# Expert weights of a mixture layer streamed in transfers of 2 MB instead of 1 MB

## What is computed

```python
def moe_swiglu(x2d, w_router, w_gate, w_up, w_down):   # 8 experts, 2 for each token
    ...
    def expert_block(args):
        xb, e = args
        return (jax.nn.silu(xb @ w_gate[e]) * (xb @ w_up[e])) @ w_down[e]
    ...
    y = jax.ops.segment_sum(y_rows[dest] * w_sorted[:, None], tok_sorted, num_segments=n_tok)
    return y.astype(x2d.dtype)

...
f = moe_swiglu(u2.reshape(b * s, d), moe_router[i // 2], moe_wg[i // 2],
               moe_wu[i // 2], moe_wd[i // 2]).reshape(b, s, d)
h = h + f
e = rms_norm(p[i] @ ple_proj[i], ple_norm_g[i])
h = h + jax.nn.sigmoid(h @ ple_gate[i]) * e
```

## Time and profile before

| | us |
|---|---|
| median of three runs | 3133.54 |
| lowest and highest | 3129.72, 3134.11 |
| the profiled execution, first to last instruction (its span) | 3126.8 |

### The profile page before, as it was taken

The page is one execution under the profiler, slowest core; times in us unless marked ns, Lnnn a source line. Parts: engine busy times, 40 slices in busy tenths (PEclk is TensorE's granted clock), DMA queues, the critical chain, the costliest instruction groups (busy, mean ns, idle before and its releaser), DMA issues. The chain is left out here.

```text
span 3126.8 us, 47318 instructions
## 1 busy us (share of the span) xinstructions
PE 3067.2 (98%) x18746; PEld 1808.6 (58%) x18746; DVE 1953.1 (62%) x3355; ACT 797.4 (26%) x2086; POOL 162.0 (5%) x146
## 2 busy tenths in 40 slices
PE   8999999999999999999999999999999999999998
PEld 7858686784468577785685576864433333333333
DVE  7766785774577544633575536432477786677777
ACT  4514452441335143221352223231200000000000
POOL 0000000000000002300001104110100000000000
PEclk9999999999999999999999999999999999999999
DMA  7442145344324440133444421133799999999993
GB/s 296 187 181 110 54 173 214 138 163 181 144 98 178 161 183 28 68 115 137 173 171 175 172 81 67 56 142 125 292 405 419 420 418 420 365 417 418 419 419 133
DMA packets 81048, 665.55 MB, mean 213 GB/s; under 512 B 10528, under 2 KB 11168, under 8 KB 14016
## 3 DMA queue, kind: packets, MB, share of 16 engines
q1 hardware_dynamic: 78816, 655.41, 52.9%
q10 hardware_dynamic: 2016, 7.13, 0.6%
HBM read 661.46 MB, written 1.05 MB: 212 GB/s over the span
## 5 line engine op out<-in xcount | busy, mean ns | idle before, releaser
L4400 PE MATMUL psum<-ring,arena 128*32 128x512 f32 x5376 | 582.2, 592 | 0.0
L4400 PEld LDWEIGHTS psum<-ring,arena 128*32 128x32 f32 x5376 | 175.3, 110 | 400.7 <-issue 399.8
L887 PE MATMUL psum<-ring,arena 128*128 128x256 f32 x1760 | 398.1, 379 | 0.8 <-DVE arena L988 0.8
L887 PEld LDWEIGHTS psum<-ring,arena 128*128 128x128 f32 x1760 | 334.1, 190 | 47.0 <-DVE ring L1001 1.2
L887 PE MATMUL psum<-ring,xT_norm 128*128 128x256 f32 x1320 | 303.0, 379 | 1.7 <-DMA ring<-in_ffn_w 1.7
L942 ACT ACTIVATE arena<-arena 32x128 f32<-32x128 f32 x880 | 269.6, 306 | 31.7 <-DVE arena L1076 22.1
L1001 DVE TENSOR_TENSOR ring<-ring 128x1024 f32<-128x1024 f32 x220 | 267.2, 1215 | 10.0 <-DMA ring<-in_ffn_w 3.4
L887 PEld LDWEIGHTS psum<-ring,xT_norm 128*128 128x128 f32 x1320 | 250.4, 190 | 35.7 <-DMA ring<-in_ffn_w 1.9
L4554 ACT ACTIVATE arena<-psum 128x256 f32<-128x256 f32 x84 | 32.5, 387 | 781.4 <-PE psum L4400 781.4
L907 PE MATMUL psum<-ring,arena 128*128 128x512 f32 x440 | 205.8, 592 | 0.0
L3253 PE MATMUL psum<-xT_norm,ring 128*128 128x256 f32 x832 | 184.1, 380 | 0.0
(11 more groups left out here) (647 smaller groups left out, 3945.3 us busy)
## 6 DMA issues: line engine op xcount, KB each, us to landing
ring<-in_moe_w SPq DMA_DIRECT2D x340, 1024.0 KB, 9.3
ring<-in_ffn_w SPq DMA_DIRECT2D x50, 2048.0 KB, 7.4
ring<-in_ffn_w SPq DMA_DIRECT2D x65, 1024.0 KB, 5.0
ring<-in_merge_w SPq DMA_DIRECT2D x16, 2048.0 KB, 8.5
ring<-in_feat_w SPq DMA_DIRECT2D x12, 2048.0 KB, 9.3
ring<-in_ev_in_w SPq DMA_DIRECT2D x4, 2048.0 KB, 8.9
ring<-in_od_in_w SPq DMA_DIRECT2D x4, 2048.0 KB, 9.6
ring<-in_merge_w SPq DMA_DIRECT2D x8, 1024.0 KB, 11.5
```

Of the source, the lines that this page charges most:

```text
L887: last = pe.matmul(psum[:, bank, 0:GROUP], a[:, k, :], w[:, k, :], start=(fresh and k == 0), stop=(k == KT // 2 - 1), skip_group_check=True)
L4400: last = pe.matmul(psum[part(j), r, :], xg[:, u.i, u.group // GROUPS, r * P + BLOCK * j:r * P + BLOCK * (j + 1)], m[:, j, :], start=(u.i = ...
```

## The change

Units are loaded two at a time: `mixture_loads` lists (first unit, count), two units where the first falls on places 0, 2, 4 or 6, one for place 8, and one for the last unit, which has no follower. `mixture_stream` lays the two units of a pair next to each other in each partition, so that one transfer brings 2 MB, 16 KB to a partition. SyncE waits for the release of the later of the two places' old units, and a pair's landing counts on the semaphore of its first place alone; TensorE and VectorE wait for that. `ple_gate` comes in two pairs in the same way, the first of which waits for both of its places.

```diff
--- before.py
+++ after.py
@@ -216,10 +216,21 @@
     return units
 
 
+def mixture_loads():
+
+    total, loads, i = len(mixture_units()), [], 0
+    while i < total:
+        n = 2 if i % UNIT_SLOTS < UNIT_SLOTS - 1 and i + 1 < total else 1
+        loads.append((i, n))
+        i += n
+    return loads + [(total, 2), (total + 2, 2)]
+
+
 def mixture_stream(gate, up, down, last):
 
 
-    out = np.empty((len(mixture_units()) + 4, P, QUAD, BANK), np.float32)
+    total = len(mixture_units()) + 4
+    out = np.empty((total, P, QUAD, BANK), np.float32)
     for at, (group, kind, i) in enumerate(mixture_units()):
         q, g = group // GROUPS, group % GROUPS
         for j in range(QUAD):
@@ -234,7 +245,8 @@
         w = pack(last[:, c * BANK:(c + 1) * BANK])
         for half in range(2):
             out[len(mixture_units()) + 2 * c + half] = w[:, 4 * half:4 * half + 4]
-    return out.reshape(-1, P, QUAD * BANK)
+    out = out.reshape(total, P, QUAD * BANK)
+    return np.concatenate([out[i:i + n].transpose(1, 0, 2).ravel() for i, n in mixture_loads()])
 
 
 def lay_out(inp):
@@ -4228,6 +4240,7 @@
 
 SHARES, TAKEN, PLACED, TABLE = 5, 12, 14, 21
 SLOT_AT = (14336, 16384, 4096, 6144, 0, 2048, 8192, 10240, 12288)
+assert all(SLOT_AT[i + 1] == SLOT_AT[i] + UNIT for i in range(0, UNIT_SLOTS - 1, 2))
 AHEAD = 4
 
 
@@ -4260,18 +4273,27 @@
         self.prog.load("router", self.router.rearrange("p k e -> p (k e)"), self.prog.inp["router"], sp)
         self.side.load_first(sp, self.mem)
 
+    def slots(self, i, n):
+        at = SLOT_AT[i % UNIT_SLOTS]
+        return self.prog.ring[:, at:at + n * UNIT]
+
+    def piece(self, i, n):
+        return self.stream[i * P * UNIT:(i + n) * P * UNIT].rearrange("(p c) -> p c", p=P)
+
     def first_units(self, sp, branch_sum):
-        for i in range(AHEAD):
+        for i in range(0, AHEAD, 2):
             if i == 2:
                 sp.wait_ge(branch_sum, 12)
-            sp.dma_start(self.slot(i), self.stream[i]).then_inc(self.prog.unit_loaded[i], 16)
+            sp.dma_start(self.slots(i, 2), self.piece(i, 2)).then_inc(self.prog.unit_loaded[i], 16)
 
     def run(self):
         prog, stream, gain, side, mem, router, slot = (
             self.prog, self.stream, self.gain, self.side, self.mem, self.router, self.slot)
         psum = prog.psum
         units = mixture_units()
+        in_pairs = stream.rearrange("(g p c) -> g p c", p=P, c=2 * UNIT)
         groups = NE // QUAD * GROUPS
+        first_of = {j: i for i, n in mixture_loads() for j in range(i, i + n)}
         loads = [len(range(s, len(units), UNIT_SLOTS)) for s in range(UNIT_SLOTS)]
         W = QUAD * BLOCK * ROUNDS
         parts = mem.take(3 * TB * D // 2).bitcast(BF16).rearrange("p (m b d) -> p m b d", m=3, b=TB)
@@ -4356,21 +4378,23 @@
             def _(sp):
                 n_passes = passes(sp)
                 with sp.Fori(0, n_passes) as k:
-                    after = sp.value_load(table[0:1, 1:1 + MAX_PASSES][:, bass.ds(k, 1)], min_val=0, max_val=len(units))
+                    after = sp.value_load(table[0:1, 1:1 + MAX_PASSES][:, bass.ds(k, 1)], min_val=0, max_val=len(units) // 2)
                     sp.wait_ge(pass_open, k + 1)
-                    for i in range(AHEAD, len(units)):
+                    for i, n in mixture_loads():
+                        if i < AHEAD or i >= len(units):
+                            continue
                         if i >= UNIT_SLOTS:
-                            wait_released(sp, k, i - UNIT_SLOTS)
-                        sp.dma_start(slot(i), stream[i]).then_inc(prog.unit_loaded[i % UNIT_SLOTS], 16)
-                    for i in range(AHEAD):
-                        wait_released(sp, k, (loads[i] - 1) * UNIT_SLOTS + i)
-                        sp.dma_start(slot(i), stream[bass.ds(after + i, 1), :, :].rearrange("g p c -> p (g c)"))\
+                            wait_released(sp, k, i + n - 1 - UNIT_SLOTS)
+                        sp.dma_start(self.slots(i, n), self.piece(i, n)).then_inc(prog.unit_loaded[i % UNIT_SLOTS], 16)
+                    for i in range(0, AHEAD, 2):
+                        wait_released(sp, k, max((loads[j] - 1) * UNIT_SLOTS + j for j in (i, i + 1)))
+                        sp.dma_start(self.slots(i, 2), in_pairs[bass.ds(after + i // 2, 1), :, :].rearrange("g p c -> p (g c)"))\
                           .then_inc(prog.unit_loaded[i], 16)
 
             @ph.block.tensor
             def _(pe):
                 def wait_unit(k, i):
-                    s = i % UNIT_SLOTS
+                    s = first_of[i] % UNIT_SLOTS
                     pe.wait_ge(prog.unit_loaded[s], k * (16 * loads[s]) + 16 * (i // UNIT_SLOTS + 1))
 
                 def gather(k, q):
@@ -4591,7 +4615,7 @@
                     last.then_inc(hidden_turned, 1)
 
                 def wait_unit(k, i):
-                    n = i % UNIT_SLOTS
+                    n = first_of[i] % UNIT_SLOTS
                     dve.wait_ge(prog.unit_loaded[n], k * (16 * loads[n]) + 16 * (i // UNIT_SLOTS + 1))
 
                 def mix_rows(k, g):
@@ -4693,8 +4717,8 @@
                 do(dve.tensor_scalar(more[:, 0:1], most, float(CAP), None, ALU.is_gt),
                    dve.tensor_scalar(more[:, 1:2], most, float(2 * CAP), None, ALU.is_gt))
                 do(dve.scalar_tensor_tensor(table_f[:, 0:1], more[:, 0:1], 1.0, more[:, 1:2], ALU.add, ALU.add),
-                   dve.tensor_scalar(table_f[:, 1:3], more, float(-len(units)), float(len(units)), ALU.mult, ALU.add),
-                   dve.tensor_scalar(table_f[:, 3:4], more[:, 0:1], 0.0, float(len(units)), ALU.mult, ALU.add))
+                   dve.tensor_scalar(table_f[:, 1:3], more, float(-len(units) // 2), float(len(units) // 2), ALU.mult, ALU.add),
+                   dve.tensor_scalar(table_f[:, 3:4], more[:, 0:1], 0.0, float(len(units) // 2), ALU.mult, ALU.add))
                 do(dve.tensor_copy(table, table_f))
                 assert do.n == TABLE, do.n
                 dve.tensor_copy(counts[:, 0:1], most).then_inc(pass_open, 1)
```

## The result

The changed kernel takes 3191.15 us (median of five runs, 3183.17 to 3208.56) where the kernel before, on the same chip, takes 3132.92 (3129.72 to 3134.11): a ratio of 1.020, 95% interval 1.0174 to 1.0223. Measured once more, in the last series of experiments, it takes 3184.87 for 3132.10, ratio 1.0176, 1.0159 to 1.0193. So it is slower by 52.8 to 58.2 us. The forecast was 3151, 17.5 us slower than its reference of 3133.54, and its range ended at 3166.

The account below looks back on a forecast made before the run. TensorE sets the pace, with the DMA 0.15 us per group faster. Terms 6.3 + 7.2 + 1.5 + 1.0 + 1.1 - 0.5 = 16.6, rounded to 17: span 3144, with 6.7 around it 3151 us; range 3136 to 3166.

Parts of the forecast that it names:

- T4 past +2.74: VectorE's weight sum T4 ending over 2.74 us after a mixed group's down part starts makes TensorE wait one for one.
- R1: Rival: in the mixture the DMA rate won lets the backlog drain and no group waits; 3132 us, chance 0.12.
- R4: Rival: engines cut 16 KB rows to 8 KB, pairs late by 0.3 us more; 3157 us, chance 0.57 together with the forecast.
- R3: Rival: strays don't count, only waits of kind C and the ends; 7.6 us, 3141 us, chance 0.12.
- R2: Rival: each pair needs 8.0 us with nothing ahead; 30 us, 3163 us, chance 0.12.
- Step (4): Lumps: queued pairs delay tight landings in the mixture, one wait of 0.9 us per three groups, 6.3 us in all.
- step (5): Strays: 0.4 us per group lost in the DMA besides the steps, three quarters counted, 7.2 us, first groups 1.5 more.
- C: Mixed groups pairing the first two and last two down units; the latter pair lands 0.9 us late.
- A: Mixed groups with the second down unit alone and the last two paired; 8.35 us to landing after C's shift, in time.
- B: Mixed groups pairing the middle two down units, and the fourth with an up unit; in time after C's shift.
- limit of 8.4: In A and C, the pair of the last two down units may take 8.4 us from issue to landing.
- The ends: Last mixed group 1.0 us and the gate's later loads 1.1 us, less half a microsecond that before already waits.

Follow-up runs that it names:

- e4: The changed kernel, but VectorE's weight sums read constants and wait for no landing; 3131.52 us, ratio 1.0002.
- e3: The changed kernel's 2 MB transfers with joint landing and later release, but from the old HBM layout in rows of 8 KB; 3190.87 us, ratio 1.0192.
- e13: The changed kernel, but the weight sums of kind C groups alone read constants and wait for no landing; 3173.72 us, ratio 1.0157.
- e1: The changed kernel's HBM layout, but transfers of 1 MB, each with its own release and semaphore; 3131.49 us, ratio 1.0001.
- e2: The changed kernel, but a pair released late goes out as two 1 MB transfers, each with its own semaphore; 3139.88 us, ratio 1.0027.
- e9: As e2, but whoever uses a unit waits for both units of its pair; 3187.23 us, ratio 1.0181.

## Why the prediction was right and wrong

**Right: the place and the chain.** In the mixture TensorE waits for VectorE's L4643 and L4657 and for nothing else of weight, the sums wait for landings, T4 past +2.74 costs one for one, the up units have room (e4), the layout is worth nothing, packets are of 16 KB, R1 doesn't come (no group ends T4 before +2.74, save the one behind the pure half). The sign and the path stand. R4 is out by e3: rows of 8 KB make no difference. R3, at 3141, is out too. R2 came nearest, 3163, with each pair 0.7 us slower from an empty queue; but what was missing isn't only there.

**Wrong: the size, 14.5 us for the 24 periods where 50.4 and 49.5 were measured, or 48 more than in before.** (14.5 is the sum's 6.3 + 7.2 + 1.5 less the half microsecond of before.) Step (4) had the state of the queue and the effect of a wait wrong, and step (5) the strays.

*Step (4), the head of C's chain "behind an idle queue".* It isn't idle. 1.5 us of work are still there, in the run where only C waits, and a surcharge of 1.4 comes on top. Where it alone waits, C is late by 2.7 to 4.0 us, not by 0.9.

*Step (4), "C's wait shifts the issues", so that A and B are in time.* In the earlier trace rows a down part takes 9.44 us; TensorE's wait falls inside it, part of it (1.26 us in the group of 2342.76) ahead of the release of d1, and all of it ahead of those of d2 and d3. So the head of the next chain is shifted along with its tight pair. In the changed kernel the next pair after 2343.0 is issued at 2351.34, 8.3 us later, in a queue that has just run dry; it takes 8.3 us for 7.3, and A's d2+d3 behind it takes 9.5 us for the limit of 8.4 (windows 2351.3:2351.5 and 2363.2:2363.4):

```profile
ring<-in_moe_w SPq DMA_DIRECT2D x1, 2048.0 KB, 8.3
...
ring<-in_moe_w SPq DMA_DIRECT2D x1, 2048.0 KB, 9.5
```

So a wait is bought back in part, where the prediction had it bought back in full. By e13, C's 18.5 us of waits take 7 to 9 us off A (24.0 without them, 14.9 and 16.8 with them) and nothing off B (16.2 without them, 16.9 and 13.9 with them, where the two traces of one kernel are 3 us apart). The rest is lost to the shifted head and to the short queue that makes the next pair dear; and with C freed A is late by 2.3 to 4.4 us in each group and B by up to 4.2, where the prediction without C's shift has 0.9.

*Step (5), strays as a rate.* The 0.4 us per group came from times to landing that rose by 1.5 us in 160 us of before, and were taken to fall at random, the same with pairs as without. They don't. On average they are larger where the queue is short, and in three traces with single transfers (before, e1, e2) it holds over 3 us of work for 832 of the 970 transfers of 1 MB. In the changed kernel's trace all surcharges together are 73 us, in before's 20. With the table in place of the rate the same arithmetic gives 44. The service of 4.88 and the 6.95 from landing to T4 stand.

*The ends.* The last mixed group was put at 1.0 us; its wait grew by 2.5 and in the repeated run by 3.4. The gate was put at 1.1 us: a wait of 3.1 where single loads leave 1.2, so 1.9, and 3.0 more where the clock fell. Group 12, at 1.6, had no term of its own.

The 6.7 us that the forecast set around the span are for the greater part a difference between runs: where time and span of one execution are both listed they are 1.8 to 1.9 us apart (3204.34 and 3202.5). The forecast loss of 17.5 us doesn't hang on it.

What stays open is the cause of the surcharge itself. The table shows when it comes and how much it is; that transfers of 1 MB in before's queue pay half of it, while those of e9 pay all, isn't explained. The packets give a hint. Most of 16 KB take 0.61 us, but from 2250 to 3090 us of the changed kernel 543 of 17,753 take over 0.5 us more, 1.49 on average, and in e4, whose queue is longer, 226 of 18,250; in before 156 of 40,961 packets of 8 KB do. The kernel counts a transfer as landed when the last of its 16 increments is in, so slow packets could be what the surcharge is made of. That is not shown, nor why they are slow. And late release with 1 MB (10 for 6) and the changed kernel (50 for 44) are a little later than calculated.

The Trainium skill, "Perfetto Trace Analysis", section DMA Optimizations, has larger DMAs as the primary optimization when DMA-bound, as they saturate the bandwidth better; its examples are of 2 to 8 KB. Here the larger transfers moved 388 GB/s in the mixture and the smaller ones 420. The larger ones moved 420 as well where nobody waited for them (e4), so it is not their rate that fell: the bytes moved depend on when places come free, and that on who waits.

## What to carry to other kernels

Two transfers made one land when the second lands and start when the second place is free; where a consumer waits for them with less than a transfer's time to spare, the size bought nothing here, and its two consequences cost more together than the sum of each alone. Before such a change, work out how much is queued at the issue of each tight transfer, not only whether bandwidth suffices: here the queue at share 1.01, seldom short, made nobody wait, and the one at 0.95, which runs short about once a group, did. And ask of a wait on the bounding engine what it delays in turn: where it delays the releases that feed the queue, it makes up for a part of itself only.

## What the runs showed of the hardware that was not expected

- A 2 MB transfer whose turn comes while under 1 us of work is queued lands on average 1.1 to 1.4 us later than its service time of 4.88 us says; with over 3 us queued, 0.0 to 0.1. The same holds for 1.75 MB (1.2 to 1.4 and 0.0, for a service of 4.27).
- Queued transfers of 1 MB (8 KB rows) and of 2 MB (16 KB rows, or 8 KB) run at the same rate within 2%: 2.49 and 2.44 us a MB, and 420 GB/s in before and in e4, where TensorE doesn't wait.
- Ahead of the mixture, TensorE's clock fell to the 1.2 GHz level for 34 and for 48 us at 2020 us in two of the profiled runs, with TensorE busy for 47.4 of 50 us in the first of them, as in before (47.7); the mixture began 17 and 23 us later than in the repeated run.
- At the gate, waits of 3.1 us at the same place were followed by 6.8 us at the 1.2 GHz level in one execution of the changed kernel and by none in the other.
